# Forget gate's group of the head stage: token-stationary form, turned by VectorE and brought round through memory, in an unrolled head loop

## The chip, the core and the metric

The kernel runs on one core of one Trainium2 chip. The metric is the device time of one execution in microseconds (us); lower is better. A core has a matrix engine (TensorE, PE in the profile; its weight loads are PEld), VectorE (DVE), ScalarE (ACT), GpSimd (POOL) and SyncE (SP), whose queue here issues nearly all DMAs.

## What is computed

A decoder trunk of two layers over 256 tokens of width 2048, in float32. The change touches the first layer's token mixer, HGRN2. Its input projection has 4 × 2048 columns: queries q, forget gate fr, values v, output gate g.

```python
proj = xn @ w_in
q, fr, v, g = jnp.split(proj, 4, axis=-1)
q = silu(q) * 128 ** -0.5
f = lb + (1.0 - lb) * sigmoid(fr)
k = 1.0 - f
logf = jnp.log(f)
o = chunked_gated_recurrence(q, k, v, logf)      # 16 heads of 128
o = rms_norm(o, out_gain) * silu(g)
return o @ w_out
```

The recurrence is S_t = diag(f_t) S_{t-1} + k_t v_t^T, o_t = S_t^T q_t. After the mixer comes a gated MLP with a causal convolution; the second layer has a short-convolution mixer and the same kind of MLP.

## The kernel before, in words

**Splitting.** Each float32 weight and activation is split into a high and a low part, and a product is three products: high × high, low activation × high weight, high activation × low weight. Weights stream from HBM in chunks of 512 KB through a ring of four slots (`raw`, `w_parts`). For each chunk ScalarE makes the high part (line 492) and VectorE the low part by a subtraction (line 769). Both do it four chunks ahead of TensorE: at chunk step c they split chunk c + 4, once TensorE has released that slot (`hi_used`, `lo_used`). SP issues the load of a chunk once VectorE's low part of the chunk four before it is done.

**Phases.** `Phase` describes each projection: iterations `n`, weight groups per iteration (512 columns each), chunks per group (`cpg`, 8 here). The head phase `HGRN_IN` has four turns; a turn works on four heads and takes four groups in the order forget gate (g = 0), queries (1), values (2), output gate (3), so 32 chunks, numbered 0 to 31 within the turn.

**Two forms.** In *feature form* the weights are stationary, and the result lies with features on partitions, as the head arithmetic wants it. A chunk is 512 rows × 256 columns: 8 matmuls of 512 columns (both parts of x side by side, line 1435) and 8 of 256 (the weights' low parts, line 1445). Two chunks run as a pair: highs of both, then lows of both. The products end in two halves of a bank, so ScalarE copies one half out (`corr`, line 499) and VectorE adds the other to it (`corrected`, line 796). In *token form* x is stationary, a chunk is 256 rows × 512 columns and 12 matmuls of 512 columns (lines 1501 to 1503), there is nothing to correct, but tokens lie on partitions; VectorE turns 32 × 32 blocks (`turn_group`, line 907), and a store to HBM (`crossing`) and four loads bring them into feature layout. The up and down projections use token form. Of the head phase, only the values stay by tokens, in a form of their own (`value_run`: the first block of 128 tokens for two chunks, then the second block); forget gate, queries and output gate are in feature form.

**Banks.** `acc` has two sets. Part a of a turn may begin when part a − 2 has been taken away (`acc_free`). A feature group has two parts, the values take a half of each set for their two token blocks.

**Head arithmetic.** VectorE scales the forget group by 1/rms (line 805), ScalarE takes the sigmoid into `tb` (line 637), VectorE makes `fpre` (the forget factor with its bound, line 1182) and the keys `kh` (line 1184). With the queries: scale, sigmoid, then `qh` (line 1199) at step (2, 0). From there VectorE works through eight levels of products (lines 1050 to 1080) and takes the results that TensorE makes from them with masked copies into `a_diag` (line 1095); `PLAN` says after which chunk TensorE runs each product. Line 1640 runs two of them: the neighbours' product after chunk 19 and the own product between the highs and the lows of the turn's last pair.

**What sets the order.** Each engine has its program written out: a body over (turn, group g, step kk) with hooks at fixed steps. On VectorE and ScalarE, `levels` and `gates_and_products` run ahead of the step's split, `corrected` and `hgrn` (as `pieces`) behind it. Before the change:

```python
if (g, kk) in ((1, 0), (2, 0)):                        # ScalarE, ahead of the split
    act_e.wait_ge(scaled_ready, at(i, HGRN_IN.scales, g))
    nc.scalar.activation(tb[:], ta[:], ACT.Sigmoid).then_inc(gate_sig, 1)
...
if kk == last and g != V_GROUP:                        # VectorE, behind the split
    scaled(i, HGRN_IN, g, min(g, V_GROUP), ta[:])
if (g, kk) == (1, 0):
    dve.wait_ge(gate_sig, at(i, 3, 1))
    # fpre for four heads, then kh
```

`loop` writes the first turn out and puts the other three into a hardware loop.

Of the kernel before, what the change touches and what calls it, by code (L numbers as in the profile page):

```python
# [26 lines left out]
P = 128  # L27
# [30 lines left out]
class Phase:  # L58


    def __init__(self, before, n, groups, k_tiles, scales=0, corrects=True, parts=2, wide_group=None):
        self.n, self.groups, self.cpg, self.parts = n, groups, k_tiles // KC, parts
        self.cpi, self.api = groups * self.cpg, groups * parts
        self.wide_group = wide_group
        wide_parts = 0 if wide_group is None else parts
        self.scales, self.corrections = scales, self.api - wide_parts if corrects else 0
# [4 lines left out]
        assert self.cpi % RING == 0 and self.c0 % RING == 0 and self.api % SETS == 0  # L71

    def wide(self, g):

        return self.parts == 1 or g == self.wide_group

    def steps(self, first, g):
# [5 lines left out]
        elif first and g == 0 and self is HGRN_IN:  # L83
            order = [(0, 0), (1, 0), (0, 1), (1, 1), (0, 2), (0, 3), (1, 2), (1, 3)]
# [7 lines left out]
    def runs(self, first, g, end):  # L92

        single = self.parts == 1 or self is HGRN_IN and first and g == 0
# [50 lines left out]
STORED_AT, FETCHED_AT = 7, 9  # L145
ADDED_AT, SQUARED_AT, NORMED_AT = 4, 5, 6
# [3 lines left out]
def loop(e, phase, body, peel_last=False):  # L150

    body(0, True)
# [10 lines left out]
def trunk(nc, x, parameters, hgrn_w_in, hgrn_w_out, sc_w_in, sc_w_out, ffn_w_up, ffn_w_down, final_norm, identity,  # L163
          level_masks, out):
    with ExitStack() as ctx:
# [118 lines left out]
        sums_stored = sem("sums_stored")  # L284
        moved_in = sem("moved_in")
# [27 lines left out]
        for phase in (UP0, DOWN0, SC_IN, UP1):  # L313
            turned_groups[phase] = groups
            groups += phase.n * phase.groups - (phase is DOWN0)
        stored_groups = {phase: n - (DT // TG - 1) * (n > turned_groups[DOWN0]) for phase, n in turned_groups.items()}

        turned_sums = pad[:, :, TAPS - 1:].rearrange("p q (b n) -> p q b n", b=T // P)
        moved_sums = tb[:].rearrange("p j t -> p (j t)").rearrange("p (b a n) -> p b a n", b=T // P, a=4)
# [24 lines left out]
        def _(sp):  # L344
# [23 lines left out]

            def cross_sums(n, kk):

                if n and kk == STORED_AT:
                    sp.wait_ge(turned_ready, turned_groups[DOWN0] + n)
                    for b in range(T // P):
                        sp.dma_start(crossing[:, b].rearrange("q p n -> p q n"), turned_sums[:, :, b]) \
                            .then_inc(sums_stored, 16)
# [71 lines left out]
            def load_first(rows):  # L447

                sp.dma_start(raw[:, 0, 0:KW // 2], rows[:, 0:KW // 2]).then_inc(first_rows_loaded, 16)
                sp.dma_start(raw[:, 0, KW // 2:], rows[:, KW // 2:]).then_inc(w_loaded[0], 16)  # L450

            sp.dma_start(h[:, 0:TW, :], x[:, 0:TW, :]).then_inc(first_x_loaded, 16)
            stream(HGRN_IN, hgrn_w_in[0], lambda i, g: i * GC + [D, 0, 2 * D, 3 * D][g])
# [30 lines left out]
        def _(act_e):  # L484
# [9 lines left out]
            def correction(i, phase, g, part, c):  # L494

                act_e.wait_ge(lo_used, at(i, phase.cpi, c + 1 + RING))
                a = g * phase.parts + part
                act_e.wait_ge(acc_free, at(i, phase.api, phase.a0 + a + SETS))
                nc.scalar.activation(corr[:], acc[:, a % SETS, :, T:], ACT.Copy).then_inc(corr_ready, 1)

            def values(i, b, c):
# [5 lines left out]
                nc.scalar.activation(vt[:, :, b, :], acc[:, b, 0, :].rearrange("p (j d) -> p j d", j=TG), ACT.Copy,  # L507
                                     scale=rs[:, T + b:T + b + 1]).then_inc(acc_free, 1)

            def phase_of(phase, pieces, peel_last=False, ahead=None):  # L510

                def body(i, first):
                    for g in range(phase.groups):
                        for kk, (part, _, _, ends) in enumerate(phase.steps(first, g)):
# [10 lines left out]
                            elif ends and phase.corrections:  # L525
# [195 lines left out]
        def _(dve):  # L721
# [17 lines left out]
            def phase_of(phase, pieces, peel_last=False, ahead=None, into=None):  # L739
                def body(i, first):  # L740
                    links[2] = 0
                    for g in range(phase.groups):
                        for kk, (part, _, _, ends) in enumerate(phase.steps(first, g)):
# [4 lines left out]
                            early = first and phase is HGRN_IN and g == 0  # L748
                            if early and ends:
                                corrected(i, phase, g, part, into(g))  # L750
                            if not last:
                                split(i, phase, c + RING)
                            if ends and phase.corrections and not early and g != phase.wide_group:
# [37 lines left out]
            def corrected(i, phase, g, part, dst):  # L791

                a = g * phase.parts + part
                skipped = phase.parts if phase.wide_group is not None and g > phase.wide_group else 0
                dve.wait_ge(corr_ready, at(i, phase.corrections, phase.corr0 + a - skipped + 1))
                v.tensor_tensor(dst[:, part * TW:(part + 1) * TW, :], acc[:, a % SETS, :, 0:T], corr[:], ALU.add) \  # L796
                    .then_inc(acc_free, 1)

            def await_corrected(i, phase, g):
                dve.wait_ge(acc_free, at(i, phase.api, phase.a0 + (g + 1) * phase.parts + SETS))  # L800
# [100 lines left out]
            def turn_group(i, phase, g, to):  # L901

                a = phase.a0 + g
                dve.wait_ge(hi_used, at(i, phase.cpi, phase.c0 + (g + 1) * phase.cpg + RING))
                dve.wait_ge(lo_used, at(i, phase.cpi, phase.c0 + (g + 1) * phase.cpg + RING))
                for b in range(T // P):
                    o = v.transpose(to[:, :, b, :], acc[:, a % SETS, b, :].rearrange("p (j q f) -> p q j f", q=4,  # L907
                                                                                        f=QUARTER))
                o.then_inc(turned_ready, 1)
                dve.wait_ge(turned_ready, at(i, phase.groups, turned_groups[phase] + g + 1))  # L910
                v.sem_inc(acc_free, 1)

            def scaled_moved(i, phase, g, dst):

                fetched = 4 * 16
                dve.wait_ge(moved_in, at(i, phase.groups * fetched, (turned_groups[phase] + g + 1) * fetched))
# [782 lines left out]
```

## Time and profile before

| | |
|---|---|
| time, median of 3 runs | 2297.32 us (2296.85 to 2297.69) |
| the profiled execution | 2296.2 us, its span 2294.4 us |
| granted TensorE clock in it | 0.999 of full speed (2.4 GHz) |
| busy: PE, DVE, ACT | 100%, 74%, 46% of the span |
| DMA | 216 GB/s mean, 461.42 MB read from HBM |
| chain that ended last | PE 92%, DVE 4%, issue 2%, ACT 1% |

The page gives shares over the whole program. The head phase is its first 404.8 us: the first turn ends at 107.9, and the other three take 99.0 us each. A timeline row merges like instructions that follow one another; its second number runs from the first's start to the last's end, and since instructions of an engine overlap a little at their ends, the time that work takes is best read from start to start.

### The profile page before, as it was taken

The page shows a single profiled execution, that of the slowest core. Times are in us where ns is not written, and L with a number is a line of the kernel's source. Part 1 is how long each engine was busy: PE and PEld are TensorE (multiplying, and loading weights), DVE is VectorE, ACT ScalarE, POOL GpSimd, SP SyncE. Part 2 cuts the span into 40 slices and gives each one's busy share as a digit, 9 for nine tenths or more (in the row PEclk, how much of TensorE's full clock was granted, in tenths as well). Part 3 has the DMA queues.
Part 4 walks back from the last instruction along what each step waited for, and adds up shares of the span by engine and source line. Part 5 has one row for each costly group of instructions (what it writes and reads, how often), then busy time and mean ns, then how long its engine had stood idle before and what let it go on. Part 6 is the DMA issues. An engine that isn't in the chain of part 4 may idle for free.

```text
span 2294.4 us, 33380 instructions
## 1 busy us (share of the span) xinstructions
PE 2283.6 (100%) x11086; PEld 1914.2 (83%) x11086; DVE 1698.3 (74%) x2135; ACT 1047.0 (46%) x1083; POOL 2.8 (0%) x9
## 2 busy tenths in 40 slices
PE   9999999999999999999999999999999999999998
PEld 8888888888888888888888888888888888888887
DVE  7979788877878888865556676766878878876554
ACT  7444444454444454444444333444444444444443
POOL 0000000000000000000000000000000000000000
PEclk9999999999999999999999999999999999999999
DMA  7555555558888888876777888667888888887754
GB/s 243 172 174 161 178 164 165 183 189 236 242 246 233 245 241 241 240 214 211 212 213 206 243 242 242 204 192 202 243 243 238 243 245 234 243 251 220 216 194 154
DMA packets 396166, 496.71 MB, mean 216 GB/s; under 512 B 18992, under 2 KB 230320, under 8 KB 395952
## 3 DMA queue, kind: packets, MB, share of 16 engines
q1 hardware_dynamic: 395072, 493.15, 72.9%
q10 hardware_dynamic: 1008, 2.43, 0.3%
q8 instruction: 52, 0.85, 0.1%
q14 instruction: 34, 0.28, 0.0%
HBM read 461.42 MB, written 31.98 MB: 215 GB/s over the span
## 4 chain that ended last, share of the span: by engine, by line
PE 92%; DVE 4%; issue 2%; ACT 1%; DMA 0%; DVEq 0%; SPq 0%; ACTq 0%
PE acc L1503 24%; PE acc L1501 24%; PE acc L1502 24%; PE acc L1435 11%; PE acc L1445 6%; DVE w_parts L769 1%; DVE a_diag L1095 1%; PE acc L1458 1%; DVE fpre L1080 1%; DVE kl L1062 0%; DMA raw<-in_hgrn_w_in 0%; PE side L1606 0%; PE acc L1466 0%; DVE ql L1056 0%; DVE ta L796 0%
## 5 line engine op out<-in xcount | busy, mean ns | idle before, releaser
L769 DVE TENSOR_TENSOR w_parts<-raw,w_parts 128x1024 fp32r<-128x1024 f32 x816 | 993.0, 1224 | 544.7 <-ACT w_parts L492 419.2
L492 ACT ACTIVATE w_parts<-raw 128x1024 fp32r<-128x1024 f32 x815 | 860.6, 1059 | 1065.7 <-PE acc L1503 838.5
L1501 PE MATMUL acc<-w_parts,xn 128*128 128x512 f32 x1728 | 672.9, 389 | 0.0
L1502 PE MATMUL acc<-w_parts,xn 128*128 128x512 f32 x1728 | 672.2, 389 | 0.0
L1503 PE MATMUL acc<-w_parts,xn 128*128 128x512 f32 x1728 | 672.2, 389 | 0.0
L1503 PEld LDWEIGHTS acc<-w_parts,xn 128*128 128x128 f32 x1728 | 324.3, 188 | 67.6
L1501 PEld LDWEIGHTS acc<-w_parts,xn 128*128 128x128 f32 x1728 | 324.3, 188 | 67.2
L1502 PEld LDWEIGHTS acc<-w_parts,xn 128*128 128x128 f32 x1728 | 324.3, 188 | 67.1
L1501 PE MATMUL acc<-w_parts,act 128*128 128x512 f32 x704 | 273.9, 389 | 0.0
L1502 PE MATMUL acc<-w_parts,act 128*128 128x512 f32 x704 | 273.9, 389 | 0.0
L1503 PE MATMUL acc<-w_parts,act 128*128 128x512 f32 x704 | 273.9, 389 | 0.0
L1435 PE MATMUL acc<-xn,w_parts 128*128 128x512 f32 x896 | 215.7, 392 | 1.5 <-ACT w_parts L492 0.7
L1435 PEld LDWEIGHTS acc<-xn,w_parts 128*128 128x128 f32 x896 | 164.5, 188 | 34.5 <-issue 0.9
L1502 PEld LDWEIGHTS acc<-w_parts,act 128*128 128x128 f32 x704 | 132.1, 188 | 27.7
L1501 PEld LDWEIGHTS acc<-w_parts,act 128*128 128x128 f32 x704 | 132.1, 188 | 27.4
L1503 PEld LDWEIGHTS acc<-w_parts,act 128*128 128x128 f32 x704 | 132.1, 188 | 27.2
L1435 PE MATMUL acc<-act,w_parts 128*128 128x512 f32 x512 | 122.7, 391 | 0.0
L1445 PEld LDWEIGHTS acc<-xn,w_parts 128*128 128x128 f32 x896 | 114.3, 191 | 4.8 <-DVE w_parts L769 0.3
L1445 PE MATMUL acc<-xn,w_parts 128*128 128x256 f32 x896 | 118.3, 284 | 0.0
L1435 PEld LDWEIGHTS acc<-act,w_parts 128*128 128x128 f32 x512 | 94.1, 188 | 18.2
L931 DVE SCALAR_TENSOR_TENSOR tb<-pad,par,tb 128x256 f32<-128x256 f32 x200 | 83.3, 478 | 0.0
L907 DVE STREAM_TRANSPOSE turned<-acc 128x512 f32<-128x512 f32 x108 | 71.0, 696 | 9.0 <-DVE tb L929 3.8
(159 smaller groups left out, 1220.2 us busy)
## 6 DMA issues: line engine op xcount, KB each, us to landing
raw<-in_ffn_w_up SPq DMA_DIRECT2D x352, 512.0 KB, 4.5
raw<-in_ffn_w_down SPq DMA_DIRECT2D x176, 512.0 KB, 4.7
raw<-in_hgrn_w_in SPq DMA_DIRECT2D x127, 512.0 KB, 3.8
raw<-in_sc_w_in SPq DMA_DIRECT2D x96, 512.0 KB, 4.6
crossing<-turned SPq DMA_DIRECT2D x54, 512.0 KB, 3.8
moved<-crossing SPq DMA_DIRECT2D x216, 128.0 KB, 4.5
raw<-in_hgrn_w_out SPq DMA_DIRECT2D x32, 512.0 KB, 3.5
raw<-in_sc_w_out SPq DMA_DIRECT2D x32, 512.0 KB, 4.7
```

What stands on the lines that cost most here:

```text
L492: nc.scalar.activation(w_parts[:, c % RING, :, 0, :], raw[:, c % RING], ACT.Copy).then_inc(hi_ready, 1)
L769: v.tensor_tensor(w_parts[:, c % RING, :, 1, :], raw[:, c % RING], w_parts[:, c % RING, :, 0, :].bitcast(F32), ALU.subtract).then_inc(lo_r ...
L907: o = v.transpose(to[:, :, b, :], acc[:, a % SETS, b, :].rearrange("p (j q f) -> p q j f", q=4, f=QUARTER))
L931: o = v.scalar_tensor_tensor(out=dst[:, j, :], in0=src, scalar=w, in1=dst[:, j, :], op0=ALU.mult, op1=ALU.add)
L1080: mark(v.tensor_tensor(pre[:, :, 1], pre[:, :, 1], pre[:, :, 0, n - 1:n].to_broadcast(shape), ALU.mult))
L1095: o = v.copy_predicated(a_diag[:].rearrange("p j b (w z n) -> p j (b w) z n", z=2, n=n)[:, :, :, 1], mask[:, None].to_broadcast([P, TG, P ...
L1435: o = mm(to[:, j, :], w[:, q, 0, j * P:(j + 1) * P], src[:, k * KW + q, :, :].rearrange("p n t -> p (n t)"), start=begin and q == 0, stop= ...
L1445: o = mm(to[:, j, T:], w[:, q, 1, j * P:(j + 1) * P], src[:, k * KW + q, 0, :], start=False, stop=end and q == KW - 1, skip_group_check=True)
L1458: o = mm(acc[:, b, 0, :], x_block(src, k * KC + q, n, b), w[:, 2 * q:2 * q + 2, 0, :], start=begin and q == 0 and n == 0, stop=False)
L1501: mm(bank, x_hi, hi, start=begin and q == 0, stop=False)
L1502: low = mm(bank, x_hi, lo, start=False, stop=False)
L1503: high = mm(bank, x_lo, hi, start=False, stop=end and q == KC - 1)
```

## The change

The forget gate's group, and it alone of the feature groups, goes to token form. `Phase` gets `token_groups`; such a group has one part instead of two, so a turn has 7 parts instead of 8. An odd number means that the bank set of a part changes from turn to turn (`acc_set`), and the head loop is written out four times instead of looped. VectorE turns the finished group into `pad` at (0, 7), ahead of that step's split; SP stores it at (1, 7) of its own order, that is behind chunk 14's load, and fetches it at (2, 1), behind chunk 16's load, into `tb`. VectorE scales it back into `pad` at (1, 4), ScalarE takes its sigmoid at (1, 5) ahead of the split, VectorE makes `fpre` and `kh` at (1, 6) behind the split. The group's two copies of corrections, two corrected sums and its scaling in `ta` fall away. In the first turn the chunks of the forget group run one by one, as before, and chunk 0 has an order of its own, all products with low weights last.

```diff
     def runs(self, first, g, end):
-        single = self.parts == 1 or self is HGRN_IN and first and g == 0
+        single = self.by_tokens(g)
...
-V_GROUP = 2
+F_GROUP, Q_GROUP, V_GROUP, GATE_GROUP = range(4)
-HGRN_IN = Phase(None, 4, 4, DT, scales=3, wide_group=V_GROUP)
+HGRN_IN = Phase(None, 4, 4, DT, scales=3, wide_group=V_GROUP, token_groups=(F_GROUP,))
...
+F_SCALED_AT, F_SIGMOID_AT, F_BOUND_AT = 4, 5, 6
...
 def loop(e, phase, body, peel_last=False):
+    if phase is HGRN_IN:
+        for i in range(phase.n):
+            body(i, i == 0)
+        return
...
+            def cross_gate(i, first, g, kk):
+                if (g, kk) == (F_GROUP + 1, STORED_AT):
+                    sp.wait_ge(turned_ready, i + 1)
+                    store_pad(heads_stored)
+                if (g, kk) == (F_GROUP + 2, FETCHED_AT - HGRN_IN.cpg):
+                    sp.wait_ge(heads_stored, (i + 1) * 16 * (T // P))
+                    fetch(moved_sums)
...
             def gates_and_products(i, g, kk):
-                if (g, kk) in ((1, 0), (2, 0)):
-                    act_e.wait_ge(scaled_ready, at(i, HGRN_IN.scales, g))
+                if (g, kk) == (F_GROUP + 1, F_SIGMOID_AT):
+                    act_e.wait_ge(scaled_ready, at(i, HGRN_IN.scales, 1))
+                    nc.scalar.activation(tb[:], scaled_gate, ACT.Sigmoid).then_inc(gate_sig, 1)
+                if (g, kk) == (Q_GROUP + 1, 0):
+                    act_e.wait_ge(scaled_ready, at(i, HGRN_IN.scales, 2))
                     nc.scalar.activation(tb[:], ta[:], ACT.Sigmoid).then_inc(gate_sig, 1)
...
+                if (g, kk) == (F_GROUP + 1, F_SCALED_AT):
+                    scaled_moved(i, HGRN_IN, 0, scaled_gate, moved_sums)
-                if kk == last and g != V_GROUP:
+                if kk == last and not HGRN_IN.wide(g):
                     scaled(i, HGRN_IN, g, min(g, V_GROUP), ta[:])
...
-                if (g, kk) == (1, 0):
+                if (g, kk) == (F_GROUP + 1, F_BOUND_AT):
                     dve.wait_ge(gate_sig, at(i, 3, 1))
...
             def levels(i, first, g, kk):
+                if (g, kk) == (F_GROUP, last):
+                    turn_group(i, HGRN_IN, g, turned_sums)
                 last_take(i, g, kk)
...
+            def first_chunk(to, src):
+                w = w_parts[:, 0]
+                products = [(n, x, y) for n in range(KC) for x, y in ((0, 0), (1, 0))] + [(n, 0, 1) for n in range(KC)]
+                for n, x, y in products:
+                    if (n, x, y) == (1, 0, 0):
+                        pe.wait_ge(hi_ready, 1)
+                    if (n, x, y) == (0, 0, 1):
+                        pe.wait_ge(lo_ready, 1 + RING)
+                    for b in range(T // P):
+                        o = mm(to[:, b, :], src[:, n, x, b * P:(b + 1) * P], w[:, 2 * n:2 * n + 2, y, :],
+                               start=(n, x, y) == (0, 0, 0), stop=False)
...
-                                if phase.parts == 1:
+                                if phase.by_tokens(g):
                                     pe.wait_ge(lo_ready, at(i, phase.cpi, c + 1 + RING))
                                     low, high = wide_tokens(to, c, src, k, begin, end)
```

How VectorE's instructions stand in the first turn, from the end of the forget group to the queries' product (the later turns have the same order there). L769, now L806, is the split of a chunk; x3 is three in a row. Before:

```order
L805 TENSOR_TENSOR ta<-ta,rs 128x1024
L769 TENSOR_TENSOR w_parts<-raw,w_parts 128x4x256
L1182 TENSOR_SCALAR fpre<-tb,one_less_lb,lb 128x256 x4
L1184 TENSOR_SCALAR kh<-fpre 128x1024
L769 TENSOR_TENSOR w_parts<-raw,w_parts 128x4x256 x3
L796 TENSOR_TENSOR ta<-acc,corr 128x512
L769 TENSOR_TENSOR w_parts<-raw,w_parts 128x4x256 x4
L796 TENSOR_TENSOR ta<-acc,corr 128x512
L805 TENSOR_TENSOR ta<-ta,rs 128x1024
L1199 SCALAR_TENSOR_TENSOR qh<-ta,tb 128x1024
```

Of the change:

```order
L806 TENSOR_TENSOR w_parts<-raw,w_parts 128x4x256 x4
L832 TENSOR_TENSOR ta<-acc,corr 128x512
L806 TENSOR_TENSOR w_parts<-raw,w_parts 128x4x256
L954 TENSOR_TENSOR pad<-tb,rs 128x8x4x32
L806 TENSOR_TENSOR w_parts<-raw,w_parts 128x4x256 x2
L1220 TENSOR_SCALAR fpre<-tb,one_less_lb,lb 128x256 x4
L1222 TENSOR_SCALAR kh<-fpre 128x1024
L806 TENSOR_TENSOR w_parts<-raw,w_parts 128x4x256
L832 TENSOR_TENSOR ta<-acc,corr 128x512
L841 TENSOR_TENSOR ta<-ta,rs 128x1024
L1239 SCALAR_TENSOR_TENSOR qh<-ta,tb 128x1024
```

`fpre` and `kh` moved from behind the split of chunk 12 to between the splits of chunks 18 and 19, and the scaling of what was brought round stands behind the split of chunk 16.

ScalarE in the same stretch, of the change (L528 is its split, L535 a copy of corrections, L664 part of the mirrored input, made in the first turn alone):

```order
L528 ACTIVATE w_parts<-raw 128x4x256
L674 ACT_TABLE_LOAD
L674 ACTIVATE tb<-pad 128x1024
L528 ACTIVATE w_parts<-raw 128x4x256
L664 ACTIVATE x_mirror<-xn 128x1024
L528 ACTIVATE w_parts<-raw 128x4x256 x2
L535 ACTIVATE corr<-acc 128x512
L664 ACTIVATE x_mirror<-xn 128x1024
L677 ACTIVATE tb<-ta 128x1024
```

The forget gate's sigmoid, line 674, now stands between the splits of chunks 16 and 17; before, it stood ahead of the split of chunk 12.

## Rows read from the trace of the kernel before

**Rows 1.** The profile's page: busy time of the TensorE, with its share and instructions

```profile
PE 2283.6 (100%) x11086; PEld 1914.2 (83%) x11086; DVE 1698.3 (74%) x2135; ACT 1047.0 (46%) x1083; POOL 2.8 (0%) x9
```

**Rows 2.** Timeline of PE, a pair of feature chunks: start us, us, engine line, op

```profile
127.39 3.82 PE L1435 MATMUL acc<-xn,w_parts 128*128 128x512 f32 x16
131.04 2.08 PE L1445 MATMUL acc<-xn,w_parts 128*128 128x256 f32 x16
132.95 1.32 PE L1435 MATMUL acc<-xn,w_parts 128*128 128x512 f32 x5
```

**Rows 3.** Timeline of PE, up projection: first matmuls of two chunks in turn

```profile
505.99 0.39 PE L1501 MATMUL acc<-w_parts,xn 128*128 128x512 f32 x1
...
508.71 0.39 PE L1501 MATMUL acc<-w_parts,xn 128*128 128x512 f32 x1
```

**Rows 4.** Timeline of DVE, second turn, queries into values (in brackets: idle before, releaser)

```profile
139.70 1.38 DVE L1182 TENSOR_SCALAR fpre<-tb,one_less_lb,lb 128x256 f32<-128x256 f32 x4
...
141.72 1.22 DVE L769 TENSOR_TENSOR w_parts<-raw,w_parts 128x1024 fp32r<-128x1024 f32 x1
...
148.96 2.36 DVE L769 TENSOR_TENSOR w_parts<-raw,w_parts 128x1024 fp32r<-128x1024 f32 x2 [2.60 <-PE acc L1445]
154.53 2.36 DVE L769 TENSOR_TENSOR w_parts<-raw,w_parts 128x1024 fp32r<-128x1024 f32 x2 [3.20 <-PE acc L1445]
156.81 0.68 DVE L796 TENSOR_TENSOR ta<-acc,corr 128x512 f32<-128x512 f32 x1
...
159.88 1.23 DVE L1199 SCALAR_TENSOR_TENSOR qh<-ta,tb 128x1024 f32<-128x1024 f32 x1 [1.13 <-ACT tb L637]
```

**Rows 5.** Timeline of ACT, same stretch: the queries' sigmoid

```profile
158.79 1.06 ACT L637 ACTIVATE tb<-ta 128x1024 f32<-128x1024 f32 x1 [2.69 <-DVE ta L805]
```

**Rows 6.** Stretch table: us, then busy us (instructions) of PE, PEld, DVE, ACT, POOL

```profile
159.88:202.92 43.04, 43.00 (x287) 35.08 (x285) 42.57 (x60) 18.66 (x21) 0.00 (x0) 1.00 0.49 152
```

**Rows 7.** Timelines of DVE and PE where that stretch ends

```profile
202.20 0.72 DVE L1095 COPY_PREDICATED a_diag<-masks,side 128x512 f32<-128x512 uint8 x1
...
202.98 1.19 PE L1640 MATMUL side<-act,sum_ones 128*128 128x512 f32 x4
```

**Rows 8.** Instructions of line 1640: what its engine sat idle for (us, times)

```profile
  DVE a_diag L1095: 2.0, 4
```

**Rows 9.** Timeline of PE, values of the second turn: the second token block begins

```profile
157.97 1.07 PE L1458 MATMUL acc<-w_parts,x_mirror 128*128 128x512 f32 x4
```

**Rows 10.** Timeline of PE, the program's first 45 us

```profile
19.72 2.11 PE L1435 MATMUL acc<-xn,w_parts 128*128 128x512 f32 x8 [0.65 <-DVE xn L825]
...
31.30 3.94 PE L1435 MATMUL acc<-xn,w_parts 128*128 128x512 f32 x16
35.08 0.67 PE L1425 MATMUL side<-sq_acc,ones 128*128 128x256 f32 x2
...
35.94 2.16 PE L1445 MATMUL acc<-xn,w_parts 128*128 128x256 f32 x16
...
44.36 3.88 PE L1435 MATMUL acc<-xn,w_parts 128*128 128x512 f32 x16 [0.69 <-ACT w_parts L492]
```

**Rows 11.** Timelines of DVE and ACT in the same 45 us

```profile
9.60 1.23 DVE L769 TENSOR_TENSOR w_parts<-raw,w_parts 128x1024 fp32r<-128x1024 f32 x1 [0.18 <-ACT w_parts L492]
...
42.21 1.06 ACT L637 ACTIVATE tb<-ta 128x1024 f32<-128x1024 f32 x1 [1.79 <-DVE ta L805]
```

**Rows 12.** Groups of DVE instructions, by form: busy us, mean ns | idle before

```profile
L907 DVE STREAM_TRANSPOSE turned<-acc 128x512 f32<-128x512 f32 x108 | 71.0, 696 | 9.0 <-DVE tb L929 3.8 <-DVE ta L929 3.8 <-PE acc L1503 1.0
L918 DVE TENSOR_TENSOR pad<-moved,rs 128x1024 f32<-128x1024 f32 x47 | 57.3, 1218 | 0.0
L1095 DVE COPY_PREDICATED a_diag<-masks,side 128x512 f32<-128x512 uint8 x28 | 24.8, 886 | 0.0
```

**Rows 13.** DMA issues of the page: KB each, median us from issue to landing

```profile
crossing<-turned SPq DMA_DIRECT2D x54, 512.0 KB, 3.8
moved<-crossing SPq DMA_DIRECT2D x216, 128.0 KB, 4.5
```

**Rows 14.** Timeline of DVE, second turn: one of the longer masked copies

```profile
173.76 1.30 DVE L1095 COPY_PREDICATED a_diag<-masks,side 128x512 f32<-128x512 uint8 x1
```

More of the change, by code:

```diff
@@ L58, with __init__ @@
 class Phase:
-    def __init__(self, before, n, groups, k_tiles, scales=0, corrects=True, parts=2, wide_group=None):
+    def __init__(self, before, n, groups, k_tiles, scales=0, corrects=True, parts=2, wide_group=None,
+                 token_groups=()):
         self.n, self.groups, self.cpg, self.parts = n, groups, k_tiles // KC, parts
[L63 to L66, printed above, removed]
+        self.wide_group, self.token_groups = wide_group, token_groups
+        self.cpi, self.api = groups * self.cpg, self.first_part(groups)
+        self.scales, self.corrections = scales, self.corrected_before(groups) if corrects else 0
+        self.turns = len(token_groups) if token_groups else groups
         self.c0 = before.c0 + before.n * before.cpi if before else 0
@@ L70, in __init__, with first_part, acc_set, corrected_before @@
         self.corr0 = before.corr0 + before.n * before.corrections if before else 0
-        assert self.cpi % RING == 0 and self.c0 % RING == 0 and self.api % SETS == 0
+        assert self.cpi % RING == 0 and self.c0 % RING == 0 and n * self.api % SETS == 0
+    def first_part(self, g):
+        return sum(1 if n in self.token_groups else self.parts for n in range(g))
+    def acc_set(self, i, a):
+        return (i * self.api + a if self.api % SETS else a) % SETS
+    def corrected_before(self, g):
+        return self.parts * sum(not self.wide(n) for n in range(g))
+    def by_tokens(self, g):
+        return self.parts == 1 or g in self.token_groups
     def wide(self, g):
-        return self.parts == 1 or g == self.wide_group
+        return self.by_tokens(g) or g == self.wide_group
     def steps(self, first, g):
@@ L284, in trunk @@
         sums_stored = sem("sums_stored")
+        heads_stored = sem("heads_stored")
         moved_in = sem("moved_in")
@@ L524, in body @@
                                 values(i, 1, c)
-                            elif ends and phase.corrections:
+                            elif ends and phase.corrections and not phase.wide(g):
                                 correction(i, phase, g, part, c)
@@ L747, in body @@
                                 ahead(i, first, g, kk)
-                            early = first and phase is HGRN_IN and g == 0
-                            if early and ends:
-                                corrected(i, phase, g, part, into(g))
                             if not last:
                                 split(i, phase, c + RING)
-                            if ends and phase.corrections and not early and g != phase.wide_group:
+                            if ends and phase.corrections and not phase.wide(g):
                                 corrected(i, phase, g, part, into(g))
@@ L791, in corrected @@
             def corrected(i, phase, g, part, dst):
[L793 to L796, printed above, removed]
+                a = phase.first_part(g) + part
+                dve.wait_ge(corr_ready, at(i, phase.corrections, phase.corr0 + phase.corrected_before(g) + part + 1))
+                v.tensor_tensor(dst[:, part * TW:(part + 1) * TW, :], acc[:, phase.acc_set(i, a), :, 0:T], corr[:], ALU.add) \
                     .then_inc(acc_free, 1)
             def await_corrected(i, phase, g):
-                dve.wait_ge(acc_free, at(i, phase.api, phase.a0 + (g + 1) * phase.parts + SETS))
+                dve.wait_ge(acc_free, at(i, phase.api, phase.a0 + phase.first_part(g + 1) + SETS))
             def scaled(i, phase, g, n, dst):
@@ L1487, in value_run @@
                             pe.wait_ge(lo_ready, at(i, HGRN_IN.cpi, c + 1 + RING))
-                            low = value_lows(c, b, src, k, end)
+                            low = value_lows(to, c, b, src, k, end)
                             if end:
```

91 lines of the change are left out of this document (47 added, 44 removed).

## The prediction

> **What bounds the kernel now.** I read the busy times on the page first: TensorE is busy 2283.6 of 2294.4 us [rows 1], with its clock granted at 0.999 throughout. So a change of form pays only by what the matmuls themselves take, and anything that makes TensorE wait costs its whole length. Next came TensorE's timeline, for the pace of each form [rows 2, 3], and then, of the waits, those of the head stage. One wait returns in all four turns of the head loop: the product of own keys and queries, line 1640, waits for VectorE's masked copy at line 1095 [rows 8]. In the second turn that copy ends at 202.20 + 0.72 = 202.92 and the matmul starts at 202.98 [rows 7]. Followed back on VectorE, the stretch from qh at 159.88 to 202.92 has 42.57 us of work in 43.04 [rows 4, 6]: it has no slack. So in every turn VectorE's work from qh to that copy sets when TensorE may go on. Whatever moves qh later, seen from TensorE's query group, moves TensorE by as much.
>
> **1. Form of the forget group.** Before, a pair of chunks takes 132.95 − 127.39 = 5.56 us, 16 matmuls of 512 columns in 3.65 and 16 of 256 in 1.91 [rows 2]. In token form a chunk has 12 of 512 columns; in the up projection that is 508.71 − 505.99 = 2.72, so 5.44 a pair [rows 3]. The columns are the same, and the gain is 0.12 a pair, **0.5 us a turn**.
>
> By the isolated gap (N/2.4 + 2.5 ns) of the Trainium skill, "TensorE: Matmul & The Clock Gate", section "Back-to-back issue gap", a pair would be 5.20 us in feature form and 5.18 in token form, 0.08 a group less. The rows differ (228 and 119 ns a matmul against its 216 and 109), so the sum goes by the rows.
>
> **2. VectorE and ScalarE in the forget group.** Out go two corrected sums, one scaling, and on ScalarE two copies of corrections. In come two transposes of 0.70 us and a scaling of 1.22 from what came back [rows 12]. I cost this at nothing: after it, in the query group, VectorE sits idle 2.60 and 3.20 us before its splits [rows 4]. The transposes stand before the split of chunk 11 and delay it by 1.5 us, but TensorE wants that low part only 5.56 + 3.65 = 9.2 us after the group's end, behind a pair and the next pair's highs. If that cover went, 4 × 1.5 would be the price.
>
> **3. The round trip.** The turned group is ready 1.4 us after the forget group ends. Its store lands in about 3.8 us and the four fetches in 4.5 more [rows 13]. SP issues them in order among the weight loads, so fetches come after chunk 16's load and hold chunk 17's by some 2 us. All is in tb about 12 us after the group's end; VectorE asks for it after chunk 16's split, at 148.96 + 1.13 = 150.1, which is 17 us after the forget group's end near 133. Weight loads behind it have as much room. Cost nothing; if that cover went, ScalarE's and VectorE's queues would stand behind the fetch.
>
> **4. The sigmoid, five chunks in.** Scaling 150.1 to 151.3, sigmoid (1.06 as at [rows 5]) to 152.4, ScalarE's split of chunk 17 to 153.4, VectorE's to 154.5. VectorE's next split, of chunk 18, may start at 154.53, when TensorE releases the slot [rows 4]. It just fits, at a cost between 0 and 0.1; I take 0.05 a turn. TensorE itself wants chunk 17 after 155.2.
>
> **5. The bound and the keys, six chunks in.** This decides. Before, lines 1182 and 1184 ran from 139.70 to 141.72, 2.02 us with idle time behind them [rows 4]. Now they are queued behind the split of chunk 18, which waits until 154.53. From there on nothing is idle until qh: split, split, corrected sum, scaling, then ScalarE's sigmoid and 1.13 us of waiting for it. So fpre and kh push chunk 19's split, the queries' last corrected sum, their sigmoid and qh by 2.02 us. The idle 3.20 us ahead of 154.53 can't take them, since they stand behind the split that waits. With the 0.05 this is **2.07 us a turn**. TensorE meets it in two places. The second token block of the values waits for the bank that the queries' last corrected sum frees: before, that ended at 156.81 + 0.68 = 157.49 and the block began at 157.97 [rows 4, 9], 0.5 in hand; now it comes at 159.55, a stall of 1.6. The rest, 0.5, is waited for at line 1640, where there was no slack.
>
> **6. The first turn.** Chunks 1 and 2 now need their low parts at once: chunk 1's is done at 9.60 + 1.23 = 10.83 [rows 11] where TensorE would be ready at 10.4. Half a microsecond is lost there and 0.25 at chunk 2, both hidden by the wait at 19.72 for the input's third part [rows 10]. From there four chunks took 31.30 − 19.72 = 11.58, the last 0.3 waiting for the bank of the gate's first part; now 4 × 2.72 = 10.88 and the queries start in the other bank: 0.70 gained. From 31.30 to 44.36 are two pairs (11.12) and the sum of squares (35.94 − 35.08 = 0.86); the other 1.08 is mostly the wait behind the sigmoid that ScalarE does at 42.21 before it splits chunk 12 [rows 10, 11]. That sigmoid is gone from there; I count 0.95. The values so begin **1.65 us** sooner. qh is late here by about as much as elsewhere: the bound and keys, 2.02, again stand between the last splits.
>
> **7. Unrolling.** The first turn is straight code already and its pairs run at the loop's pace; from line 1095's end to the next turn's first matmul both kinds take the same. Nothing for it, below or above.
>
> **Sum.** First turn −1.65 + 2.05 = +0.4. Three turns of −0.5 + 2.07 = +1.57 give +4.7. Together +5.1 us. The profiled execution took 2296.2 (its span 2294.4), so 2301.3 by it; the median of the runs is 1.1 higher, so **2302.4**. Bounds: part 4 0 to 0.1 a turn; part 6 ±1; where qh's delay is paid, 1.9 to 2.2 a turn. The forecast's own range is 2300.5 to 2304.5. A measurement here tells 0.2% (4.6 us) from no change, and the forecast lies just beyond it.
>
> **Rivals.**
> - **Faster: VectorE's lateness is taken up.** If the stretch behind qh had slack over 2 us, only the gains stay: −1.65 − 3 × 0.5 = −3.15, **2294.2**. It decides where the delay that reaches TensorE falls under 0.8 us a turn (3.15 / 4). For it: TensorE's wait at line 1640 is only 2.0 us in four times now. Against: 42.57 busy in 43.04. Chance 0.13; part of it is not past the 0.2% line.
> - **Half of it hidden.** Two of seven masked copies last 1.30 where the others take 0.72 (mean 0.886 of 28) [rows 12, 14]. If they stretch by waiting for TensorE, a late VectorE finds them short and wins back 2 × 0.58 of the 2.07, leaving 0.9 a turn: 4 × 0.9 − 3.15 = +0.5, **2297.8**. Against: the mean fits 1.30 and 0.72 exactly in every turn. Other partial recoveries come to the same. Chance 0.20.
> - **More is late.** Part 4 fits by less than 0.1; if ScalarE's splits or the fetch slip by 1 us a turn (the fetch shares the DMA with weight loads), qh slips by the same: +4, **2306.4**. Chance 0.12.
> - **The form gains next to nothing.** If a chunk's pace is not the up projection's but leaves 0.1 a turn, the sum is 1.6 higher: **2304.0**. That is also what the page's gap named under 1 would make of it. Rows 3 speak against it. Chance 0.05.
>
> **How the numbers follow.** The forecast has 0.50. About half of that lies past +4.6 us (0.27), the rest within. Slower: 0.27 + 0.12 + 0.05 = 0.44. Same: 0.23 + 0.20, and a little of the faster case, 0.44. Faster: 0.12. The range 2295.5 to 2307 leaves out the faster case and a tail above, under 0.2 together.
>
> **What the new profile would show.** Forget chunks every 2.72 us; in each turn TensorE idle some 1.6 us before the values' second block, released by the corrected sum of the queries, and again before the own product; VectorE's fpre and kh directly between the splits of chunks 18 and 19, no idle time from there to qh but for the sigmoid; a turn 100.5 us long instead of 99.0; the values of the first turn begun near 53.9 instead of 55.55. Wrong would be: no wait at the second block, idle time on VectorE between qh and the own product's copy, or a wait for the fetch.

## Result, and the profile after

The changed kernel takes **2302.94 us** (median of 10, 2301.47 to 2304.07), the kernel before 2296.76 (10 runs, 2296.12 to 2297.69) on the same chip: a ratio of 1.0027, 95% interval [1.0017, 1.0037]. It is slower by 6.2 us, where 5.1 was forecast: 0.3%, small, but clear of no change. A second series of it, on another chip, gave 1.0029 [1.0017, 1.0042].

The profiled execution, first the span and the busy times (answers to [rows 1]):

```profile
span 2301.6 us, 32392 instructions
PE 2282.9 (99%) x10958; PEld 1908.2 (83%) x10958; DVE 1699.8 (74%) x2135; ACT 1042.3 (45%) x1075; POOL 2.8 (0%) x9
```

TensorE's busy time is 0.7 us lower and the span 7.2 longer: what was added is mostly waiting, and some matmuls at a lower clock, which count as busy (below). All waits of TensorE that the trace puts down to an engine (us in total, times, longest):

```profile
PE acc L1496 <- DVE ta L832: 8.1, 4, 3.7
PE side L1691 <- DVE a_diag L1131: 1.4, 3, 0.5
PE side L1643 <- POOL ones L514: 1.1, 1, 1.1
PE acc L1541 <- DVE w_parts L806: 0.4, 1, 0.4
```

The first line is new: the values' second token block (line 1496, which was 1458) waits in each of the four turns for the corrected sum of the queries (line 832). The second is the own product. [rows 8] had that wait in four turns, as the weight load of line 1640 saw it; between the matmuls themselves this view had 0.5 us once before, in the first turn, and has it now in the three later ones. TensorE in the second turn (start us, us, in brackets idle time before and releaser):

```profile
110.11 0.47 PE L1541 MATMUL acc<-w_parts,xn 128*128 128x512 f32 x1
...
156.93 2.00 PE L1496 MATMUL acc<-w_parts,xn 128*128 128x512 f32 x8
158.77 1.07 PE L1504 MATMUL acc<-w_parts,xn 128*128 128x512 f32 x4
161.29 1.20 PE L1496 MATMUL acc<-w_parts,x_mirror 128*128 128x512 f32 x4 [1.45 <-DVE ta L832]
...
206.83 0.94 PE L1691 MATMUL side<-act,sum_ones 128*128 128x512 f32 x3 [0.47 <-DVE a_diag L1131]
```

Of the kernel before, the first matmuls of the second turn, of its values and of what follows the head stage, beside [rows 7, 9]:

```profile
107.88 3.92 PE L1435 MATMUL acc<-xn,w_parts 128*128 128x512 f32 x16
...
155.22 2.00 PE L1458 MATMUL acc<-w_parts,xn 128*128 128x512 f32 x8
...
404.80 3.92 PE L1435 MATMUL acc<-act,w_parts 128*128 128x512 f32 x16
```

The brackets show 1.45 us at the second block and 0.47 at the own product; forecast were 1.6 and 0.5. Read from start to start, the second block begins 161.29 − 156.93 = 4.36 us after the values, where it was 157.97 − 155.22 = 2.75, so 1.61 later, and the own product 206.83 − 156.93 = 49.90, where it was 202.98 − 155.22 = 47.76, so 2.14 later. VectorE in the same turn, beside [rows 4]:

```profile
151.82 1.22 DVE L954 TENSOR_TENSOR pad<-tb,rs 128x1024 f32<-128x1024 f32 x1
155.11 2.36 DVE L806 TENSOR_TENSOR w_parts<-raw,w_parts 128x1024 fp32r<-128x1024 f32 x2 [2.08 <-ACT w_parts L528]
157.39 1.38 DVE L1220 TENSOR_SCALAR fpre<-tb,one_less_lb,lb 128x256 f32<-128x256 f32 x4
158.81 0.69 DVE L1222 TENSOR_SCALAR kh<-fpre 128x1024 f32<-128x1024 f32 x1
159.41 1.22 DVE L806 TENSOR_TENSOR w_parts<-raw,w_parts 128x1024 fp32r<-128x1024 f32 x1
160.55 0.68 DVE L832 TENSOR_TENSOR ta<-acc,corr 128x512 f32<-128x512 f32 x1
...
163.62 1.23 DVE L1239 SCALAR_TENSOR_TENSOR qh<-ta,tb 128x1024 f32<-128x1024 f32 x1 [1.13 <-ACT tb L677]
```

The bound and the keys stand between the splits of chunks 18 and 19, and from 155.11 on nothing is idle but for the sigmoid. qh comes 163.62 − 156.93 = 6.69 us after the values' start, where it was 159.88 − 155.22 = 4.66: **2.03 later**, forecast 2.02. The stretch from qh to the own product's copy is what it was (stretch table, columns as in [rows 6]), and so are the longer masked copies:

```profile
163.62:206.69 43.07, 42.74 (x286) 34.85 (x284) 42.59 (x60) 18.89 (x21) 0.00 (x0) 1.00 0.51 149
```

```profile
177.50 1.30 DVE L1131 COPY_PREDICATED a_diag<-masks,side 128x512 f32<-128x512 uint8 x1
```

The turns begin at 110.11, 210.68 and 311.24, and what follows them at 411.79: each takes **100.56** (before 98.97, from 107.88 to 404.80 three of them; forecast 100.5). The first turn ends at 110.11 instead of 107.88, **+2.23**, where +0.4 was forecast. There the numbers part:

```profile
53.30 2.00 PE L1496 MATMUL acc<-w_parts,xn 128*128 128x512 f32 x8
55.14 1.07 PE L1504 MATMUL acc<-w_parts,xn 128*128 128x512 f32 x4
59.95 1.20 PE L1496 MATMUL acc<-w_parts,x_mirror 128*128 128x512 f32 x4 [3.75 <-DVE ta L832]
60.99 0.71 PE L1504 MATMUL acc<-w_parts,x_mirror 128*128 128x512 f32 x2
61.50 1.91 PE L1496 MATMUL acc<-w_parts,x_mirror 128*128 128x512 f32 x4
```

The wait is 3.75 us, and behind it four matmuls of 512 columns take 1.91 us instead of 1.07. The stretch table has the granted clock (the figure after the five engines):

```profile
56.05:59.95 3.90, 0.16 (x1) 0.00 (x0) 3.83 (x9) 1.20 (x2) 0.00 (x0) 1.00 0.76 243
59.95:61.50 1.55, 1.55 (x7) 1.24 (x7) 1.21 (x1) 0.31 (x1) 0.00 (x0) 0.96 0.58 81
61.50:64.06 2.56, 2.56 (x8) 1.97 (x6) 1.74 (x2) 1.70 (x2) 0.00 (x0) 0.50 0.41 156
64.06:67.17 3.11, 3.11 (x14) 2.54 (x13) 3.02 (x6) 1.59 (x2) 0.00 (x0) 0.88 0.00 0
```

TensorE resumed at 59.95; from some 61.4 to 64.8 us its clock was granted at 0.50, that is 1.2 GHz instead of 2.4.

### The profile page after: what moved, and what is told of

Same layout as the page of the kernel before. It is cut to its first block, busy times and chain, and to the rows that moved or that the text cites. A ratio compares the mean times of both kernels' runs of the same rounds, so it can differ in the third digit from the quotient of the medians.

```text
span 2301.6 us, 32392 instructions
## 1 busy us (share of the span) xinstructions
PE 2282.9 (99%) x10958; PEld 1908.2 (83%) x10958; DVE 1699.8 (74%) x2135; ACT 1042.3 (45%) x1075; POOL 2.8 (0%) x9
## 4 chain that ended last, share of the span: by engine, by line
PE 91%; DVE 5%; issue 2%; ACT 1%; DMA 0%; SPq 0%; DVEq 0%; ACTq 0%
PE acc L1541 25%; PE acc L1543 25%; PE acc L1542 25%; PE acc L1473 9%; PE acc L1483 5%; DVE w_parts L806 2%; PE acc L1496 1%; DVE fpre L1116 1%; PE side L1657 0%; DVE kl L1098 0%; DVE ql L1092 0%; DVE a_diag L1131 0%; ACT w_parts L528 0%; PE acc L1504 0%; DMA raw<-in_hgrn_w_in 0%
## 5 line engine op out<-in xcount | busy, mean ns | idle before, releaser
L806 DVE TENSOR_TENSOR w_parts<-raw,w_parts 128x1024 fp32r<-128x1024 f32 x816 | 993.6, 1224 | 550.2 <-ACT w_parts L528 433.3
L528 ACT ACTIVATE w_parts<-raw 128x1024 fp32r<-128x1024 f32 x815 | 860.2, 1059 | 1078.8 <-PE acc L1543 891.2
L1541 PE MATMUL acc<-w_parts,xn 128*128 128x512 f32 x1852 | 721.9, 390 | 0.4 <-DVE w_parts L806 0.4
L1543 PE MATMUL acc<-w_parts,xn 128*128 128x512 f32 x1852 | 720.6, 389 | 0.0
L1542 PE MATMUL acc<-w_parts,xn 128*128 128x512 f32 x1852 | 720.5, 389 | 0.0
L1541 PEld LDWEIGHTS acc<-w_parts,xn 128*128 128x128 f32 x1852 | 347.6, 188 | 73.1 <-issue 1.1
L1542 PEld LDWEIGHTS acc<-w_parts,xn 128*128 128x128 f32 x1852 | 347.7, 188 | 72.1
L1543 PEld LDWEIGHTS acc<-w_parts,xn 128*128 128x128 f32 x1852 | 347.6, 188 | 72.1
L1473 PE MATMUL acc<-xn,w_parts 128*128 128x512 f32 x640 | 152.8, 391 | 0.0
L1473 PEld LDWEIGHTS acc<-xn,w_parts 128*128 128x128 f32 x640 | 118.1, 188 | 23.6
L1483 PE MATMUL acc<-xn,w_parts 128*128 128x256 f32 x640 | 84.3, 285 | 0.0
L1483 PEld LDWEIGHTS acc<-xn,w_parts 128*128 128x128 f32 x640 | 81.0, 191 | 3.0
```

The lines of the kernel that those rows point to most:

```text
L528: nc.scalar.activation(w_parts[:, c % RING, :, 0, :], raw[:, c % RING], ACT.Copy).then_inc(hi_ready, 1)
L806: v.tensor_tensor(w_parts[:, c % RING, :, 1, :], raw[:, c % RING], w_parts[:, c % RING, :, 0, :].bitcast(F32), ALU.subtract).then_inc(lo_r ...
L1473: o = mm(to[:, j, :], w[:, q, 0, j * P:(j + 1) * P], src[:, k * KW + q, :, :].rearrange("p n t -> p (n t)"), start=begin and q == 0, stop= ...
L1483: o = mm(to[:, j, T:], w[:, q, 1, j * P:(j + 1) * P], src[:, k * KW + q, 0, :], start=False, stop=end and q == KW - 1, skip_group_check=True)
L1541: mm(bank, x_hi, hi, start=begin and q == 0, stop=False)
L1542: low = mm(bank, x_hi, lo, start=False, stop=False)
```

## The experiments

Three questions: which part costs the turns' 1.6 us and which gives; what the unrolling does; and what happened in the first turn. The theory is the prediction's: the bound and the keys behind the split of chunk 18. Line numbers in the rows are each kernel's own.

**Unrolling alone.** The kernel before, its head loop written out:

```diff
+    if phase is HGRN_IN:
+        for i in range(phase.n):
+            body(i, i == 0)
+        return
```

> The kernel before, with the head loop written out four times and nothing else. My theory (VectorE's lateness is the cost, unrolling is free): the three later turns stay at 99.0 us, the time within 0.5 us of the kernel before. Rival (straight code has to be fetched and costs something): each of the three later turns over 99.3 us, the time 1 to 5 us more.

Measured 2297.29 (11 runs) against 2296.57, ratio 1.0003 [0.9994, 1.0012]. A product near each turn's end begins at 108.19, 207.27, 306.29 and 405.36, so turns of 99.08, 99.02 and 99.07 against 98.97. Straight code costs 0.1 us a later turn at most; the median's 0.7 us is a little more than the 0.5 expected and inside the interval. The first turn of that execution ended 1.2 us late, since ScalarE waited 0.91 us for chunk 18's weights; why they were late there stays open.

**The late bound alone.** The kernel before in feature form, only the bound and the keys moved to six chunks in:

```diff
-                if (g, kk) == (1, 0):
+                if (g, kk) == (1, 6):
```

> The kernel before, all groups in their old form, with fpre and kh alone moved from (1, 0) to (1, 6), behind the split of chunk 18. My theory: the three later turns go from 99.0 to 101.0 us, idle time before the values' second block and a longer wait before the own product; the first turn 2.0 us longer as well; in all 8.1 us more than before, about 2304.9, up to 1.5 more if the clock falls in the first turn's wait. Rival (VectorE has slack behind qh and the form or the round trip is the cost): turns stay within 0.3 us of 99.0, the time within 1.5 us of before.

Measured 2303.45 (7 runs), ratio 1.0029 [1.0017, 1.004], 6.9 us slower where some 8 was expected; the profiled execution, the slowest of the seven, took 2304.11. Its waits:

```profile
PE acc L1458 <- DVE ta L796: 5.8, 4, 1.4
PE side L1640 <- DVE a_diag L1095: 1.6, 4, 0.5
```

One position on VectorE's queue brings both waits, with no round trip and no token form: turns begin at 109.58, 210.59 and 311.60, 101.01 each. That is 2.04 more than 98.97, within 0.02 the duration of those five instructions. Its first turn ends 1.70 late, and behind a wait of 1.44 us there the clock stayed at 1.00.

**The same form, bound and keys a place or two earlier.** The changed kernel with the scaling, the sigmoid and the bound asked for at chunks 3, 4 and 4, and the sigmoid behind ScalarE's split of that chunk:

```diff
-F_SCALED_AT, F_SIGMOID_AT, F_BOUND_AT = 4, 5, 6
+F_SCALED_AT, F_SIGMOID_AT, F_BOUND_AT = 3, 4, 4
@@ ScalarE, behind the split
+                if (g, kk) == (F_GROUP + 1, F_SIGMOID_AT):
+                    act_e.wait_ge(scaled_ready, at(i, HGRN_IN.scales, 1))
+                    nc.scalar.activation(tb[:], scaled_gate, ACT.Sigmoid).then_inc(gate_sig, 1)
```

> The changed kernel with the forget gate worked out earlier: scaling at (1, 3), sigmoid at (1, 4) behind ScalarE's split instead of ahead of one, fpre and kh at (1, 4) behind the split of chunk 16. Form, turning and round trip are as in the change. My theory: VectorE does the 2.02 us in idle time, qh is not late, the three later turns take 98.5 us (0.5 less than before), the first turn ends within 0.5 us of 107.6; about 2295.0, 1.8 us less than before. Rival (form and round trip cost the time by themselves): turns stay at 100.5 us, the time at 2302.9. A third: the fetch is not back by then in the later turns, VectorE waits for it at (1, 3), turns between 99 and 100.5.

Measured 2294.51 (11 runs), ratio 0.9991 [0.9982, 1.0], so barely told from no change against the kernel before, but 8 us below the changed one. Turns of 98.53, as expected; the first ends at 108.62, outside the 0.5 us around 107.6 that were expected. The bound now has idle time behind it, as before the change:

```profile
150.32 1.38 DVE L1220 TENSOR_SCALAR fpre<-tb,one_less_lb,lb 128x256 f32<-128x256 f32 x4
151.74 0.69 DVE L1222 TENSOR_SCALAR kh<-fpre 128x1024 f32<-128x1024 f32 x1
152.35 1.22 DVE L806 TENSOR_TENSOR w_parts<-raw,w_parts 128x1024 fp32r<-128x1024 f32 x1
154.75 2.36 DVE L806 TENSOR_TENSOR w_parts<-raw,w_parts 128x1024 fp32r<-128x1024 f32 x2 [1.18 <-PE acc L1483]
```

So the loss of the three later turns is the place, not the round trip or the form. The wait at the second block remains in the first turn alone, 2.14 us, since VectorE there stands 4.64 us for the fetch. The same kernel ran a second time, under the label u7_twice_kh:

> The kernel with the early sigmoid once more, beside the all-early one on the same chip: turns of 98.5 us and 2294.5 as before; the difference to the all-early kernel lies in the first turn alone. Rival: the two differ in the later turns too.

It gave 2294.18 (8 runs), ratio 0.9989 [0.9979, 0.9999], turns of 98.47. The same 2.14 us wait was followed by a granted clock of 0.50 from some 59.2 to 62.7 us in the first profile and of 1.00 throughout in the second. In the first series four of 11 executions, the profiled one among them, have spans of 2293.6 to 2294.3 (three with a mean clock of 0.998 over the program), the other seven 2292.0 to 2292.9 at 0.999; in the second all 8 have 0.999 and 2291.7 to 2293.0. The profiled one of the first series is the fourth, with the half clock in its first turn and a mean of 0.999: a mean of 0.999 doesn't rule out a fall.

**Filling the first turn's wait.** The changed kernel, with 14 matmuls of 512 columns into an unused place between the values' two token blocks of the first turn; nobody reads what they compute:

```diff
+                            if first and b == 1:
+                                for _ in range(14):
+                                    mm(side[:, 1, 0:2 * T], src[:, 0, 0, 0:P],
+                                       src[:, 0, :, :].rearrange("p n t -> p (n t)"), start=True, stop=True)
```

> The changed kernel with 14 matmuls of 512 columns whose result nobody reads, put in the first turn between the values' first and second token block, where TensorE sits idle 3.75 us. My theory: the idle time is what lets the granted clock fall to half at 61.5 us; filled, the clock stays at 1.0 through 59 to 67 us and the first turn ends 1.2 to 1.6 us sooner (second turn's first matmul at 108.6 instead of 110.1), the time about 2301.4. Rival (the slow stretch has another cause): no difference, 2302.9.

Measured 2302.41 (10 runs), ratio 1.0025 [1.0015, 1.0034], with the clock at 1.00 in this stretch:

```profile
61.50:64.06 2.56, 2.56 (x13) 2.12 (x12) 2.39 (x3) 1.02 (x2) 0.00 (x0) 1.00 0.09 33
```

Thirteen matmuls where the changed kernel had eight in the same 2.56 us. From the second block's start to behind the pair product it takes 68.06 − 59.27 = 8.79 us against 70.34 − 59.95 = 10.39, so the low clock took 1.6. The second turn began at 108.66, as expected. Yet the time was 1.0 above the 2301.4 expected, and the two medians, from different chips, lay only 0.5 apart. So the changed kernel, this one and one with half the matmuls (`range(7)`) ran side by side on one chip.

> The changed kernel once more, on the chip of the two kernels with added matmuls. The first series of its executions carried a mean clock of 0.998 or 0.997 in nine of ten, where the kernel with 14 added matmuls carried 0.999 in all ten, but the two medians differed by 0.5 us of span only and came from different chips. If the clock falls after the wait of 3.75 us in the first turn and costs 1.6 us, nearly all spans here lie 1 to 2 us above those of the kernel with 14 matmuls run beside it (some 2301.3 against 2300). If the cost is seldom paid, the two medians agree within 0.4.

> The changed kernel with 14 unread matmuls in the first turn's wait before the values' second token block, for the comparison on one chip. By the theory of the clock 1.0 to 1.6 us below the changed kernel; by the rival within 0.4 of it. The mean clock is 0.999 in all executions either way.

> The same with 7 unread matmuls (1.6 us) directly behind the first token block, so that TensorE still sits idle for 3.75 - 1.6 = some 2.1 us. The kernel with the sigmoid early had a wait of 2.14 us there, and the clock fell in 4 of its first 11 executions (0.998) and in none of the 8 of its second series. If the length of the idle time alone decides, it is the same mix here: the median lies near that of the 14 matmuls, with some executions 1 to 2 us above. If what decides is that TensorE is idle at all there, the median lies with the changed kernel.

Measured in turn: 2304.12 (6 runs, ratio 1.0029), 2301.96 (11 runs, 1.0023 [1.0014, 1.0032]) and 2301.52 (10 runs, 1.0023 [1.0013, 1.0032]). The changed kernel carried a mean clock of 0.997 in four executions (spans 2302.2 to 2302.7), 0.998 in one (2300.2) and 0.999 in one (2299.4); the 14 matmuls 0.999 in all 11, the 7 matmuls 0.999 in nine of ten. The profile of the 7 shows a wait of 1.75 us, not the 2.1 expected. In the changed kernel's new profile the wait was 4.13 us, and the half clock began before TensorE resumed, at some 58.7, and lasted to 65.5:

```profile
59.00:61.50 2.50, 1.20 (x3) 1.01 (x4) 2.46 (x3) 0.00 (x0) 0.00 (x0) 0.50 0.60 188
61.50:64.00 2.50, 2.50 (x8) 1.93 (x7) 1.34 (x3) 2.00 (x2) 0.00 (x0) 0.50 0.45 170
```

What it costs at the end of the first turn is told by qh, which is known for each. The kernel before has qh at 60.83 and the end at 107.88:

```profile
55.48 2.36 DVE L769 TENSOR_TENSOR w_parts<-raw,w_parts 128x1024 fp32r<-128x1024 f32 x2 [0.67 <-ACT w_parts L492]
...
60.83 1.23 DVE L1199 SCALAR_TENSOR_TENSOR qh<-ta,tb 128x1024 f32<-128x1024 f32 x1 [1.13 <-ACT tb L637]
```

The profiled execution of each kernel, in us against that:

| kernel | idle before block 2 | qh | end of first turn | clock behind the wait |
|---|---|---|---|---|
| changed | 3.75 | +1.45 | +2.23 | 0.50 |
| changed, again | 4.13 | +1.80 | +3.38 | 0.50 |
| 14 matmuls | 0.22 | +0.77 | +0.78 | 1.00 |
| 14 matmuls, again | 0.97 | +1.55 | +1.54 | 1.00 |
| 7 matmuls | 1.75 | +0.70 | +0.67 | 1.00 |
| unrolled alone | 1.13 | +1.18 | +1.19 | 1.00 |
| late bound alone | 1.44 | +1.71 | +1.70 | 1.00 |
| a place or two earlier | 2.14 | −0.04 | +0.74 | 0.50 |
| the same, again | 2.14 | −0.42 | −0.44 | 1.00 |
| everything early (below) | none | −3.53 | −3.54 | 1.00 |

With the clock held, the turn is late by what qh is late, within 0.03 us in seven profiles, as the prediction's first paragraph has it. With the clock at half, 0.8, 1.6 and 0.8 us come on top. The rival that the cost is seldom paid falls: on one chip the median of the spans is 2302.3 against 2300.2 with the 14 matmuls. So does the one that any idle time there will do: with the 7 matmuls the median lies with the 14, not with the changed kernel, though two of its ten executions are 1.4 and 1.8 us above it.

**Everything early.** The places 3, 4, 4 again, but now SP issues the fetch before chunk 16's load instead of behind it, and sigmoid, bound and keys stand ahead of their engines' splits of that chunk:

```diff
-                if (g, kk) == (F_GROUP + 2, FETCHED_AT - HGRN_IN.cpg):
+                if (g, kk) == (F_GROUP + 2, 0):
```

> The changed kernel with everything of the forget gate as early as it goes: SP fetches at (2, 0) ahead of chunk 16's load, scaling at (1, 3), sigmoid ahead of ScalarE's split at (1, 4), fpre and kh at (1, 4) ahead of VectorE's split. My theory: later turns 98.5 us as with the early sigmoid; in the first turn the fetch is back some 4 us sooner, so the values' second block finds its bank free or nearly, the clock stays at 1.0, and the second turn begins near 105.7 instead of 108.6; about 2291.6, 5 us less than the kernel before. Rival (in the first turn it is the weight loads, not the order, that hold the queries' last splits): the second turn still begins at 107 to 108.6, time about 2294.

Measured **2291.92** (11 runs, 2291.52 to 2292.55), ratio 0.9979 [0.997, 0.9988]: it beats both kernels. TensorE, first turn, then VectorE, second turn:

```profile
54.48 1.07 PE L1504 MATMUL acc<-w_parts,xn 128*128 128x512 f32 x4
55.39 1.07 PE L1496 MATMUL acc<-w_parts,x_mirror 128*128 128x512 f32 x4
```

```profile
144.57 1.39 DVE L1229 TENSOR_SCALAR fpre<-tb,one_less_lb,lb 128x256 f32<-128x256 f32 x4 [1.13 <-ACT tb L674]
145.99 0.69 DVE L1231 TENSOR_SCALAR kh<-fpre 128x1024 f32<-128x1024 f32 x1
146.60 2.35 DVE L806 TENSOR_TENSOR w_parts<-raw,w_parts 128x1024 fp32r<-128x1024 f32 x2
150.48 2.36 DVE L806 TENSOR_TENSOR w_parts<-raw,w_parts 128x1024 fp32r<-128x1024 f32 x2 [1.52 <-PE acc L1483]
```

No wait at the second block in any turn. The first turn ends at 104.34, sooner than the 105.7 expected and 3.54 sooner than before, and the others take 98.54; 3.54 + 3 × 0.43 = 4.8 us, and 4.7 are measured. The run changes the fetch's place and the order ahead of the splits together; how much of the first turn's gain belongs to each is not shown.

## Why the prediction was right, and where it was not

The forecast was 2302.4 and the sum +5.1; measured are 2302.94 and +6.2. By the trace the head stage ends at 411.79 instead of 404.80, +6.99: three turns +4.76 (forecast 4.71), the first +2.23 (forecast 0.4). The medians differ by less than the traces, since the profiled execution before lay 0.56 below its median and the new one 0.44 above. That the forecast came within 0.5 of the time is luck in part: it took the median 1.1 above the profiled execution, from three runs, where ten give 0.56, and so had half a microsecond too much there against 1.1 too little in the sum. The stated range, 2295.5 to 2307, holds the old time as well; it is the turns and waits that test the mechanism.

1. **Form: right.** From a turn's start to the values' start are 156.93 − 110.11 = 46.82 us, where it was 155.22 − 107.88 = 47.34: 0.52 less, forecast 0.5. Turns without the late bound take 98.53, which is 0.44 under 98.97. The prediction's estimate of 0.08 from the isolated gap of the Trainium skill, "TensorE: Matmul & The Clock Gate", section "Back-to-back issue gap", does not fit this.
2. **VectorE and ScalarE in the forget group: right.** In the second turn TensorE waits for nothing there.
3. **The round trip: right in three turns, not in the first.** The four fetches are issued from 141.28 and land 5.1 us later; VectorE asks at 151.8. In the first turn ScalarE's split of chunk 16 waited 2.32 us for its weights, and VectorE stood 0.29 us for the fetch.
4. **Sigmoid five chunks in: right in three turns.** The split of chunk 18 follows at 155.11 + 1.14 = 156.25; by the old place less 0.52, TensorE releases its slot 46.13 after the turn's start, at 156.24. It fits with nothing lost (0.05 a turn was in the sum).
5. **Bound and keys: right**, in place, size (2.03) and both payments (1.61 to the second block's start and 0.53 from there to the own product, 2.14 in all). That this alone does it is shown by the kernel before with the bound moved, and by the one that moves it back.
6. **The first turn: wrong.** The step that failed is "qh is late here by about as much as elsewhere": the term of 2.05 measured 3.70. The values began at 53.30, 2.25 sooner than before where 1.65 was forecast, but qh came at 62.28, 1.45 later, where the terms say 0.4. The splits did not keep up with the values: VectorE's split of chunk 18 began at 54.91, only 0.57 sooner than before (55.48). With 2.02 for bound and keys that gives the 1.45. In the second turn it began at 156.25, 0.7 us ahead of the values; here it was 1.6 behind them. That difference of 2.3 is 1.15 from chunk 16, whose weights ScalarE waited for, 0.38 from the fetch, for which VectorE then stood (0.29 of it idle), and 0.75 from the piece of the mirrored input that ScalarE makes between its splits of chunks 17 and 18. The values' extra 0.6 comes mostly from chunk 4: it began at 19.24 instead of 19.72 and did not wait for the input, whose third part VectorE had done at 18.98 instead of 19.67. So the 0.41 us lost at chunk 1 is there and did not reach chunk 4, but there was no wait left to hide it in. The first turn's queries:

```profile
49.72 1.23 DVE L954 TENSOR_TENSOR pad<-tb,rs 128x1024 f32<-128x1024 f32 x1 [0.29 <-DMA tb<-crossing]
53.02 1.23 DVE L806 TENSOR_TENSOR w_parts<-raw,w_parts 128x1024 fp32r<-128x1024 f32 x1 [2.07 <-ACT w_parts L528]
54.91 1.22 DVE L806 TENSOR_TENSOR w_parts<-raw,w_parts 128x1024 fp32r<-128x1024 f32 x1 [0.67 <-ACT w_parts L528]
56.06 1.38 DVE L1220 TENSOR_SCALAR fpre<-tb,one_less_lb,lb 128x256 f32<-128x256 f32 x4
```

   Values that begin early and a sum that comes late make the wait long, and the long wait brought the low clock, for which the sum had no term: another 0.8 us in this execution and 1.6 in the other one profiled.
7. **Unrolling: right** in size, 0.1 us a later turn at most.

The rivals. Lateness taken up: no, VectorE's stretch still has 42.59 us of work in 43.07. Half hidden: no, the longer masked copies still take 1.30. More is late: not in each turn, but its mechanism, splits and fetch that slip, is part of what happened in the first. The form gains nothing: no, 0.52 us to the values' start.

## What to carry to other kernels

Work that is put on an in-order queue behind an instruction that waits for a slot cannot use the idle time ahead of that wait. With nothing idle behind it, it costs its whole duration (2.02 us of work, 2.04 a turn here); with idle time behind it, nothing (turns of 98.53): look for the idle time behind the place, not in front of it. Check a schedule that just fits in the steady turn again in the first turn, where one-off work and queued loads share the engines. When a result travels through memory, try issuing its fetch ahead of the next load, and all that uses it ahead of the next split: here the two together turned +6.2 us into −4.7.

## What the hardware showed that was not expected

- Idle time in the middle of full work cost more than itself. With waits of 3.75 and 4.13 us the granted clock stood at 0.50 (1.2 GHz) until 64.8 and 65.5 us, and 1.6 us of TensorE's work time were lost by it in the first profile. It fell 1.4 us after TensorE had resumed in the first and 1.6 us before in the second. Of the changed kernel's 16 executions 14 have a mean clock of 0.998 or 0.997.
- With a wait of 2.14 us it fell in one profile and not in another of the same kernel. With 1.75 us, and with the 1.45 us of the later turns, it stayed at 1.00 in the profiles. The two stretches with 2.14 us are not quite alike: from the start of the four matmuls ahead of the wait to the second block are 58.46 − 54.92 = 3.54 us in the one and 58.07 − 54.77 = 3.30 in the other. Whether that separates them is open. Unread matmuls in the gap kept the clock up, and the median fell by 2.2 us on one chip (2304.12 to 2301.96), part of which may be the spread of the first turn's loads.
- The first turn's fetch and loads vary by up to 0.8 us from execution to execution (the queries' last sum at 59.22 and 59.57 in the changed kernel, 58.53 and 59.31 with the 14 matmuls), the later turns keep their length within 0.03 us (100.54 to 100.57 in both profiles).
